# Ranking the last eight experts by their counts: four whole, four in pairs of 64 slots

## The reference

```python
def moe_swiglu(h, w_router, w_gate, w_up, w_down):
    t = h.reshape(bsz * seq, d)                      # 256 x 1024
    logits = (t @ w_router).astype(jnp.float32)      # 256 x 8
    top_vals, top_idx = lax.top_k(logits, TOP_K)     # 2 of 8
    top_w = jax.nn.softmax(top_vals, axis=-1)
    gates = jnp.sum(jax.nn.one_hot(top_idx, N_EXPERTS_2) * top_w[..., None], axis=1)
    out = jnp.zeros_like(t)
    for e in range(N_EXPERTS_2):
        out = out + gates[:, e:e + 1] * swiglu(t, w_gate[e], w_up[e], w_down[e])
```

## Time and profile before

| | |
|---|---|
| runs, median (lowest to highest) | 2430.45 us (2424.09 to 2430.66) |
| span of the profiled execution | 2418.4 us |
| median above that span | 12.05 us |
| PE busy | 2120.8 us (88%) |
| DVE busy | 1428.3 us (59%) |
| ACT busy | 1153.2 us (48%) |
| bytes moved by DMA | 663.11 MB, mean 274 GB/s |

### The profile page before, as it was taken

The page is one execution under the profiler, slowest core; times in us unless marked ns, Lnnn a source line. Parts: engine busy times, 40 slices in busy tenths (PEclk is TensorE's granted clock), DMA queues, the critical chain, the costliest instruction groups (busy, mean ns, idle before and its releaser), DMA issues.

```text
span 2418.4 us, 30590 instructions
## 1 busy us (share of the span) xinstructions
PE 2120.8 (88%) x12751; PEld 1649.4 (68%) x12751; DVE 1428.3 (59%) x1962; ACT 1153.2 (48%) x1460; POOL 46.6 (2%) x110
## 2 busy tenths in 40 slices
PE   7989988986556666989999987899999999999997
PEld 7968767742111122668998886778888888888885
DVE  3844655421111102335555756669989989989997
ACT  4433255300000001344444576557787787777775
POOL 0000200000000000000000000000000000000000
PEclk9989999997887777999999988999999999999999
DMA  8453751789999999494554532449999989989994
GB/s 268 162 197 105 246 190 70 283 342 409 409 409 409 409 409 371 162 360 167 187 192 158 166 136 96 144 149 339 347 356 338 380 320 347 377 334 363 337 347 177
DMA packets 225353, 663.11 MB, mean 274 GB/s; under 512 B 17924, under 2 KB 26664, under 8 KB 224948
## 3 DMA queue, kind: packets, MB, share of 16 engines
q1 hardware_dynamic: 217452, 652.91, 72.1%
q10 hardware_dynamic: 7752, 8.11, 1.1%
HBM read 659.90 MB, written 1.10 MB: 273 GB/s over the span
## 4 chain that ended last, share of the span: by engine, by line
PE 64%; DMA 16%; DVE 11%; ACT 5%; issue 2%; POOL 0%; ACTq 0%; DVEq 0%; POOLq 0%; SPq 0%
PE psum L263 16%; PE psum L264 16%; PE psum L265 16%; PE psum L252 6%; DMA ring<-in_w_expert_up 5%; DMA ring<-in_w_expert_down 5%; DMA ring<-in_w_expert_gate 5%; PE psum L2453 2%; DVE w_lo L202 2%; ACT w_hi L192 1%; DVE xbc L919 1%; PE psum L1120 1%; PE psum L259 1%; PE psum L2475 1%; DMA ring<-in_ada_w 1%
## 5 line engine op out<-in xcount | busy, mean ns | idle before, releaser
L202 DVE TENSOR_TENSOR w_lo<-ring,w_hi 128x1024 fp32r<-128x1024 f32 (+1 forms) x778 | 898.7, 1178 | 341.1 <-ACT w_hi L192 328.7
L192 ACT CAST w_hi<-ring 128x1024 fp32r<-128x1024 f32 (+1 forms) x778 | 785.6, 1016 | 429.8 <-PE psum L265 425.4
L263 PE MATMUL psum<-w_hi,xg_hi 128*128 128x512 f32 (+1 forms) x768 | 291.0, 379 | 1.4 <-ACT xg_lo L2102 1.3
L265 PE MATMUL psum<-w_lo,xg_hi 128*128 128x512 f32 (+1 forms) x768 | 290.2, 378 | 0.0
L264 PE MATMUL psum<-w_hi,xg_lo 128*128 128x512 f32 (+1 forms) x768 | 289.9, 378 | 0.0
L2453 PE MATMUL psum<-ring,hT 128*32 128x512 f32 x960 | 157.0, 788 | 105.3 <-DMA ring<-in_w_expert_gate 58.2
L2453 PEld LDWEIGHTS psum<-ring,hT 128*32 128x32 f32 x960 | 30.8, 126 | 222.9 <-issue 82.5
L263 PEld LDWEIGHTS psum<-w_hi,xg_hi 128*128 128x128 f32 x768 | 145.2, 189 | 31.4 <-ACT xg_lo L2102 1.4
L265 PEld LDWEIGHTS psum<-w_lo,xg_hi 128*128 128x128 f32 x768 | 145.0, 189 | 29.0
L264 PEld LDWEIGHTS psum<-w_hi,xg_lo 128*128 128x128 f32 x768 | 145.1, 189 | 28.4
L2284 DVE TENSOR_TENSOR x<-x,psum 128x1024 f32<-128x1024 f32 x14 | 17.1, 1221 | 215.8 <-PE psum L252 215.8
(11 more groups left out here) (668 smaller groups left out, 3758.4 us busy)
## 6 DMA issues: line engine op xcount, KB each, us to landing
ring<-in_moe_w_down SPq DMA_DIRECT2D x40, 2048.0 KB, 10.2
ring<-in_w_expert_gate SPq DMA_DIRECT2D x32, 2048.0 KB, 17.2
ring<-in_moe_w_gate SPq DMA_DIRECT2D x32, 2048.0 KB, 9.6
ring<-in_moe_w_up SPq DMA_DIRECT2D x32, 2048.0 KB, 9.3
ring<-in_w_expert_down SPq DMA_DIRECT2D x30, 2048.0 KB, 17.4
ring<-in_w_expert_up SPq DMA_DIRECT2D x28, 2048.0 KB, 17.3
ring<-in_ada_w SPq DMA_DIRECT2D x24, 2048.0 KB, 11.8
ring<-in_moe_w_gate SPq DMA_DIRECT2D x16, 1536.0 KB, 6.5
```

What stands on the lines that cost most here:

```text
L192: a.copy(self.buffers(n, src.shape)[0], src).then_inc(*self.hi_made.up())
L202: v.tensor_tensor(lo, src, hi.bitcast(F32), SUB).then_inc(*self.lo_made.up())
L263: p.matmul(o, l[0], r[0], start=start, stop=False)
L265: return p.matmul(o, l[0], r[1], start=False, stop=stop)
```

## The change

Only the last expert stage is changed. DVE sorts the experts by their counts (`order_dve`) and rearranges places and gates by rank (`ranked_dve`). Ranks 0 to 3 (the four largest) are heavy: 128 slots and split weights as before. Ranks 4 and 5, and 6 and 7, are light pairs (numbered 4 and 5): each expert has 64 slots, the two of a pair stand side by side in the 128 rows of PSUM, and their weights are multiplied as f32 straight from the ring. The order is written out in `PHASES`; "in" is gate and up, "out" is down:

```diff
+SIDE = P // 2
+HEAVY = 4
+RANKS = {0: (0,), 1: (1,), 2: (2,), 3: (3,), 4: (4, 5), 5: (6, 7)}
+PHASES = (("in", 0), ("out", 0), ("in", 4), ("in", 1), ("out", 1), ("out", 4),
+          ("in", 2), ("out", 2), ("in", 5), ("in", 3), ("out", 3), ("out", 5))
```

SP loads nothing of this stage until the order is known; then it reads the experts' numbers from SBUF at the head of each "in" and loads by them. The units of a light pair alternate between its two experts:

```diff
-        ring.load(s, len(ring.units))
-        for k, e, _ in over_cases(s, run2, over2):
+        ring.load(s, units_moe2)
+        s.wait_ge(*S["moe2"].dve.of("order"))
+        experts = {}
+        for phase, i in PHASES:
+            if phase == "in":
+                for r in RANKS[i]:
+                    experts[r] = s.value_load(moe2.order[0:1, r:r + 1], min_val=0, max_val=7)
+            ring.load(s, units_after[phase, i], experts)
+        for k, e, _ in over_cases(s, run2, over2, weights=True):
```

```diff
+    def order_dve(v, st, M, counts):
+        d = st.dve
+        settle(v, v.scalar_tensor_tensor(M.key[:, :], counts, 8.0, M.iota[:, :], MUL, SUB), d)
+        settle(v, v.max(M.top[:, :], M.key[:, :]), d)
+        settle(v, v.max_index(M.order[:, :], M.top[:, :], M.key[:, :]), d, "order")
+
+    def ranked_dve(v, st, M):
...
+        settle(v, v.tensor_copy(M.order_f[:, :], M.order[:, :]), d)
+        settle(v, v.tensor_tensor(M.chosen[:, :, :], M.iota[:, :].unsqueeze(1).to_broadcast([P, n, n]),
+                                  M.order_f[:, :].unsqueeze(2).to_broadcast([P, n, n]), ALU.is_equal), d)
...
+        for values, ranked in ((M.all_pos, M.pos), (M.all_gates, M.gate)):
+            for t in range(NT):
+                v.tensor_tensor(picked[:, t, 0:n, :], values[:, t, :].unsqueeze(1).to_broadcast([P, n, n]), M.chosen[:, :, :],
+                                MUL).then_inc(*d.up())
+            v.wait_ge(*d.last())
+            settle(v, v.tensor_reduce(ranked, picked[:, :, 0:n, :], AX.X, ADD), d, "ranked")
```

The products of a light pair, and the wait and the release of both slots around each pair of units (those of "out" are alike, 4 row blocks and two halves of 512 columns):

```diff
+    def light_in_product_pe(p, i, g, ch, ps, cuts):
...
+            for u in sides:
+                p.wait_ge(*ring.loaded(u))
+            for k in range(moe2.kper):
+                for cut in cuts:
+                    for side in range(2):
+                        r = slice(SIDE * side, SIDE * side + SIDE)
+                        ins = p.matmul(ps[r, cut], moe2.xg_pair[:, i - HEAVY, k0 + k, r], w[side][:, k, cut], start=k0 + k == 0, stop=k0 + k == KD - 1)
+            ins.then_inc(*st.pe.up("unit", sides[1]))
+            for u in sides:
+                ring.empty(st.pe, u)
```

```diff
+    def in_pe(p, i):
+        st = S["moe2"]
+        held = phase_before("in", i)
+        for ch, n in enumerate(moe2.chunks):
...
+                if ch == 0 and g == 0:
+                    if i == 0:
+                        constant_products(p, ps, ident, 16)
...
+                (heavy_in_product_pe if i < HEAVY else light_in_product_pe)(p, i, g, ch, ps, cuts)
+                if g == 0:
+                    if ch == 0 and held[0] == "out":
+                        scatter_pe(p, run2, held[1])
+                    if turned_in(i, ch):
+                        mid_pe(p, run2, *turned_in(i, ch))
+                if i == 0 and ch == 1:
+                    light_step_pe(p, g)
...
+    def in_act(a, i):
...
+        if i >= HEAVY:
+            split.make_hi(a, parts_ahead("in", i, PARTS))
...
+    def out_pe(p, i):
...
+            if k0 == 4:
+                if light:
+                    scatter_pe(p, run2, out_before(i))
+                else:
+                    mid_pe(p, run2, i, len(M.chunks) - 1)
+                selgT_pe(p, run2, i)
...
+            if i == HEAVY and 4 <= k0 <= 16:
+                pair_step_pe(p, 1, k0 // 4 - 1)
```

The conversions of the stage's first parts under `ssm_out` and the norm are taken out, and the limit from which a second pass is needed becomes 64 tokens for light experts (`ranked_table_dve`, in place of `table_dve`, done during the first light "in"):

```diff
-        split.make_hi(a, split_ends[1] + PARTS)
+        split.make_hi(a, split_ends[1])
...
-                split.make_lo(v, split_ends[1] + 2)
...
-        split.make_lo(v, split_ends[1] + 3)
-        norm_dve(v, st, xn_moe, ss_moe, modulated_gain(1), modulated_shift(1), None,
-                 beside=lambda: split.make_lo(v, split_ends[1] + 4))
+        norm_dve(v, st, xn_moe, ss_moe, modulated_gain(1), modulated_shift(1), None)
...
+        v.tensor_scalar(M.over[:, 0:HEAVY], top[:, 0:HEAVY], 8.0 * P, None, ALU.is_gt).then_inc(*d.up())
+        settle(v, v.tensor_scalar(M.over[:, HEAVY:n], top[:, HEAVY:n], 8.0 * SIDE, None, ALU.is_gt), d)
```

More of the change, by code:

```diff
@@ L2166, in expert_pe @@
-                if g == 0 and ch == 0:
-                    after_gate()
+                    p.wait_ge(*st.dve.of("xg", i))
+                    p.wait_ge(*run.ring.loaded(u))
+                    w = run.ring.slot(u)[:, 0:M.kper * n].rearrange("p (k n) -> p k n", k=M.kper)
+                    for k in range(M.kper):
+                        for cut in cuts:
+                            ins = p.matmul(ps[:, cut], M.xg[:, k0 + k, :], w[:, k, cut], start=k0 + k == 0, stop=k0 + k == KD - 1)
+                    ins.then_inc(*st.pe.up("unit", u))
@@ L2201, in hi_after @@
-    def hi_after(a, run, u):
-        if run.three:
-            run.split.make_hi(a, min(run.split.end(u) + PARTS, split_ends[2]))
-    def lo_after(v, run, u):
-        if run.three:
-            run.split.make_lo(v, min(run.split.end(u) + PARTS, split_ends[2]))
+            p.wait_ge(*run.ring.loaded(u))
+            w = run.ring.slot(u)[:, 0:kn * D].rearrange("p (k n) -> p k n", k=kn)
+            for k in range(kn):
+                for half in range(2):
+                    cut = slice(half * 512, (half + 1) * 512)
+                    ins = p.matmul(ps[:, cut], M.midT[:, k0 + k, :], w[:, k, cut], start=k0 + k == 0, stop=k0 + k == M.n_k - 1)
@@ L2209, in mid_act @@
+            ins.then_inc(*st.pe.up("unit", u))
+            run.ring.empty(st.pe, u)
     def mid_act(a, run, i, ch):
@@ L2343, in y_lo_dve, with chunk_before, turned_in @@
         run.banks.empty(st.dve, st.name, "down", i)
-    def nothing(*_):
-        pass
-    def experts_pe(p, run, over):
-        n = run.moe.n_exp
-        def beside(step):
-            if i % 2 and i + 1 < n and step < 4:
-                pair_step_pe(p, i // 2 + 1, step)
+    IN_CHUNKS = [(i, ch) for i in INS for ch in range(len(moe2.chunks))]
+    def chunk_before(i, ch):
+        n = IN_CHUNKS.index((i, ch))
+        return IN_CHUNKS[n - 1] if n else None
+    def turned_in(i, ch):
+        b = chunk_before(i, ch)
+        return b if b and (ch or b[0] >= HEAVY) else None
@@ L2387, in experts_dve, with ranked_experts_dve @@
+    def ranked_experts_dve(v):
         pair_select_dve(v, 0)
[L2388 to L2391 removed]
+        for phase, i in PHASES:
+            (in_dve if phase == "in" else out_dve)(v, i)
+        scatter_dve(v, run2, OUTS[-1])
+        over_dve(v, run2, over2)
     def over_pe(p, run, over):
@@ L2395, in over_pe @@
             gather_pe(p, over, k)
[L2396 removed]
+            expert_pe(p, over, k)
             scatter_pe(p, over, k)
@@ L2407, in over_dve, with over_cases @@
             gather_dve(v, over, k)
-            expert_dve(v, over, k, e, slots, nothing)
+            expert_dve(v, over, k, e, slots)
             scatter_dve(v, over, k)
-    def over_cases(e, run, over, first=None, alone=None):
+    def over_cases(e, run, over, first=None, alone=None, weights=False):
         M = run.moe
```

473 lines of the change are left out of this document (325 added, 148 removed).

## The result

The changed kernel takes 2406.07 us (median of 4 runs, 2404.29 to 2407.14) for 2427.27 us before (4 runs, 2422.96 to 2430.66): ratio 0.9916, 95% interval 0.9897 to 0.9935. It is faster, as forecast, but by 21 us (0.8%) where 83 were forecast, and it lies 11 us above the range.

A forecast was written before the change was run, and what follows sets the result against it. TensorE was taken to bound the last expert stage, with the loads the next limit. Stage terms summed to 2322 us, 13 for the light stages' cycle made 2335, and 12.05 around the span made 2347 us; range 2320 to 2395.

The forecast's parts named there:

- The bound now and the work removed: Last expert stage: TensorE bounds it; a light pair costs 113.5 us of TensorE for 185.4 before.
- Rival (b): Light stages: tiles of 64 columns don't run side by side; 2510 us, slower by 80; chance 0.06.
- The stream's full rate: Last expert stage: loads reach 409 GB/s, a 2 MiB unit in 5.12 us, all eight experts in 676 us.
- Rival (a): Last expert stage: the stream gives no more than now, 350 GB/s; 2430 us, no change; chance 0.05.
- light stages at 350 GB/s: Light stages: sign that would show the stream giving no more than now.
- The start: Stage start: SyncE waits for the order of the counts; first product at 1616.5 for 1610.7, +5.8 us.
- The price of the light stages' own cycle: Light stages: a pair's round takes 9.75 of 10.24 us; overruns of 5 us and slow starts of 8 add 13.
- The lead of 17 us: End of a heavy expert: the ring of four slots lets loads run ahead by about 17 us of stream.
- The clock: Light stages: a start at 1.2 GHz lengthens 6.9 us of products by up to 1.7; 8 us in all.
- rival (c): Light stages: the clock stays low and turns take 10 us each; 2416 us, still faster by little; chance 0.05.
- The 12.05 us around the span: Outside the span: the runs' median lies 12.05 us above the profiled span, kept on top of 2335.
- rival d: Last expert stage: a light expert with over 64 tokens takes its own pass, about 115 us; 2466; chance 0.02.

The follow-up runs named there:

- run 1: Changed kernel with both experts of a light pair in one slot (two 1 MiB loads), each slot given back singly; 2357.53 us, ratio 0.9721.
- run 9: Changed kernel with the stage's ring cut into 16 slots of 512 KiB, a pair still given back together; 2334.74 us, ratio 0.9641.
- run 5: run 1 with TensorE waiting for two slots before it multiplies either, slots still given back singly; 2359.68 us, ratio 0.9737.
- run 7: Changed kernel with two zero products ahead of each wait for a light pair's units; 2400.13 us, ratio 0.9905.
- run 6: run 5 with both slots given back together after the second; 2393.46 us, ratio 0.9865.

## Why the prediction was wrong, step by step

Stage by stage in us, turns included (first product of one stage to that of the next; the last one to its last product):

| stage | forecast | changed kernel | run 1 | run 9 |
|---|---|---|---|---|
| heavy 0 | 100.2 | 99.9 | 99.3 | 99.4 |
| light 4 in | 103.2 | 122.0 | 109.9 | 103.5 |
| heavy 1 | 96.7 | 97.4 | 97.9 | 96.4 |
| light 4 out | 45.8 | 65.6 | 53.9 | 46.0 |
| heavy 2 | 97.8 | 99.7 | 98.8 | 99.1 |
| light 5 in | 103.2 | 124.5 | 110.5 | 102.7 |
| heavy 3 | 96.7 | 96.4 | 98.3 | 97.4 |
| light 5 out | 42.7 | 57.8 | 48.4 | 44.3 |

- **The bound now and the work removed: right.** TensorE bound the stage; the heavy stages came out within 2 us of their sums, and a burst at 7.09 for 6.9. (One reading was off without harm: the 48% of the earlier trace rows are not all of this stage. By the prediction's own 92.7 us, eight experts are 742 us, 31% of the span; the same lines also run in earlier stages.) Rival (b), tiles of 64 one after the other, is refuted: it wanted 13.7.
- **The stream's full rate: right.** 404 to 409 GB/s is there whenever a slot is free. (The Trainium skill's limit of about 358 GB/s, "DMA: Bandwidth & Descriptors", Specifications, is passed by each of these full-rate rows.) Rival (a) is refuted as a mechanism, though its 350 GB/s is what the light stages show: the mean of full rate and of stops. The sign named for (a), "light stages at 350 GB/s", does not tell it from slots that come back late; windows of a microsecond or less do.
- **The start: about right.** The order is known at 1607.2 and the first product comes at 1618.53 (forecast 1604.5 and 1616.5; the router itself ran 2.5 us later in this execution). From the order to the first issue, with the register read, it takes 1.1 us, for 1.2 that had been taken without a row. For the earlier trace rows, the timeline:

```profile
1607.05 0.16 DVE L2098 FIND_INDEX8 order<-top,key 128x8 uint32<-128x8 f32 x1
...
1608.34 0.99 SPq L139 DMA_DIRECT2D ring<-in_moe_w_gate  x2
...
1618.53 0.47 PE L263 MATMUL psum<-w_hi,xg_hi 128*128 128x512 f32 x1 [0.39 <-DVE w_lo L202]
```

- **The price of the light stages' own cycle: this step failed.** The mechanism stood in the prediction; the size of its term was wrong. "9.75 of the 10.24" put the landing at 0.75 us, from a unit loaded alone. At the two stops read above it is 0.9 and 2.2 us in the running stream, since the last part of a unit can trail, and 2.3 us pass until the bytes flow, for 2.1. So a round is up to 11.6 for 9.75 at the full clock. About every second burst was slow on top, in the first light "in" by 1.3 to 2.2 us; the forecast had counted "up to 1.7" for half of the pairs, and of that only half of what passes the slack. (That half is 0.6 us and not 0.65, which changes nothing.) The stream stops in nearly every cycle of two pairs, for 3.6 us at the stop shown. 13 us were put; the four light stages came out 75 us above their other terms (122.0 - 103.2 + 65.6 - 45.8 + 124.5 - 103.2 + 57.8 - 42.7), and the stream lost 60 us in them. Run 9, with slots of a quarter of the size, comes within 1.6 us of these other terms in all. That is in part luck: its lead is longer than forecast, and its stream still lost 14 us by the sum of 0.25 us windows.
- **The lead of 17 us: somewhat too much, and not all of it is of use.** By bytes it was 14.8 us. The ring was full at 1724, but the first light pair gave its slots back only at 1725.58. The forecast has no term for this stop; by the same sum it costs 2.2 to 2.8 us at the head of each light stage, 10 in all. The window of the changed kernel from there to the first new bytes:

```profile
1724.00:1728.00 4.00, 2.99 (x16) 1.00 (x14) 0.00 (x0) 0.00 (x0) 0.00 (x0) 1.00 0.41 114
```

- **The clock: seen, and its price is only known in part.** In the first light "in" every other burst started at 1.2 GHz, after gaps of 2.7 to 5.9 us, and took 8.4 to 9.3 us for 7.1 (rival (c) spoke of such, and of turns of 10 us, which took 0.5 to 5.6). Run 5 shows that with slots given back singly this hides (2 us). With slots given back together a slow burst keeps them shut for longer, so clock and release work on each other; run 7 gives back 6 us net of what its zero products cost, where the intervals of the two ratios overlap. The share of the clock under the joint release stays open.
- **The 12.05 us around the span: wrong**, 1.7 by the run's own time. It made the forecast of the time too high and hid 8.5 of the 67.6 us of the miss.
- **No second pass (rival d):** after the last scatter only the final norm and the store follow, 20.7 us for 19.2 from the last product to the end.

The miss of 67.6 us is thus 62 in the light stages (75 less the 13 put), 2 at the start, 2 in the heavy stages and 1.5 behind the last product. Of the 48.5 us between the changed kernel and run 1, 34 are the release (run 5 to 6), 13 the layout of loads (changed kernel to run 6), 2 the waiting by twos; each holds to some 5 us, since the kernel before moved by that much from set to set (2422.08 to 2427.27).

## What to carry to other kernels

A ring's slots count by the time that they stay shut: late last bytes, work, release and new bytes, against the loading time of the other slots. Where several slots are given back together, work out this loop with the landing of a running stream, not that of a lone transfer, and with the longest burst, not the usual one. Cut the slots smaller before adding work elsewhere. A mean rate below the peak does not tell a slow stream from one that stops; short windows do.

## What was not expected of the hardware

- The last bytes of a unit in a running stream can trail: after the bulk, 30 GB/s for 1.5 us, and 2.2 us to the products.
- Loads of 512 KiB (one row block of 128 x 1024) kept 406 GB/s with 16 slots, within 1% of the 409 of 2 MiB loads.
- Addresses read from a register at run time cost the loads nothing that shows: in the changed kernel a pair's products began 12.85 us after its issue (1725.58 to 1738.43), 2.6 more than its bytes take; a lone unit from a fixed address landed in 7.7, also 2.6 more.
